# The powers of a block-diagonal inverse held as 16 columns a row, spread to 128 behind the last product

## What is computed

```python
def rwkv7_scan(r, decay, k, v, kk, a):
    def step(S, inp):
        r_t, w_t, k_t, v_t, kk_t, a_t = inp
        sa = jnp.einsum('bhij,bhj->bhi', S, -kk_t)
        S = (S * w_t[:, :, None, :]
             + sa[..., None] * (kk_t * a_t)[:, :, None, :]
             + v_t[..., None] * k_t[:, :, None, :])
        y = jnp.einsum('bhij,bhj->bhi', S, r_t)
        return S, y
```

## Time and profile before

| what | value |
|---|---|
| median of 3 runs | 1010.13 us (1010.09 to 1010.5) |
| the profiled execution | 1011.37 us, span 1009.5 us |
| TensorE matmuls | 942.1 us busy, 93% |
| TensorE weight loads | 847.1 us, 84% |
| VectorE | 574.7 us, 57% |
| ScalarE | 452.3 us, 45% |
| GpSimd | 74.9 us, 7% |
| granted TensorE clock, mean | 0.977 |
| the inverse's products | about 381 to 445 us |

### The profile page before, as it was taken

One profiled execution on the slowest core, in us unless ns is written; L12 is line 12 of the kernel. 1 busy time (PEld: TensorE's weight loads), 2 busy tenths in 40 slices (PEclk: granted clock), 3 DMA queues, 4 the chain that ended last, 5 costly groups with the idle time before them and its releaser, 6 DMA issues.

```text
span 1009.5 us, 16945 instructions
## 1 busy us (share of the span) xinstructions
PE 942.1 (93%) x7262; PEld 847.1 (84%) x7262; DVE 574.7 (57%) x706; ACT 452.3 (45%) x621; POOL 74.9 (7%) x150
## 2 busy tenths in 40 slices
PE   4999999998979998999899999997999699999995
PEld 3898889998779987887689999996985589999994
DVE  4456677556567767735475555546541865555553
ACT  5445555434356644430264444444521654435441
POOL 6000000000120012000000000000542000000000
PEclk9999999999899999989999999998999899999998
DMA  9754444556544551000155565654772156556521
GB/s 304 241 172 147 146 144 150 167 169 207 178 151 150 181 168 43 2 1 2 43 167 195 188 202 168 203 184 130 222 225 79 61 177 201 188 191 202 170 84 42
DMA packets 105642, 152.52 MB, mean 151 GB/s; under 512 B 4050, under 2 KB 82272, under 8 KB 105568
## 3 DMA queue, kind: packets, MB, share of 16 engines
q1 hardware_dynamic: 101120, 141.45, 43.2%
q0 software_dynamic: 4272, 9.85, 3.5%
q10 hardware_dynamic: 176, 0.14, 0.0%
HBM read 145.58 MB, written 1.06 MB: 145 GB/s over the span
## 4 chain that ended last, share of the span: by engine, by line
PE 85%; DVE 5%; ACT 4%; issue 3%; DMA 1%; POOL 0%; POOLq 0%; SPq 0%; ACTq 0%; DVEq 0%
PE banks L1671 23%; PE banks L1672 23%; PE banks L1673 23%; PE banks L2006 4%; PE banks L2205 3%; DVE wl L1035 2%; ACT wh L625 1%; PE banks L2094 1%; DMA raw<-in_w_in 1%; PE banks L1784 1%; DVE xl L1083 1%; PE banks L2105 1%; DMA arena<-in_l_rel_bias 1%; PE banks L1808 1%; PE banks L1759 1%
## 5 line engine op out<-in xcount | busy, mean ns | idle before, releaser
L1035 DVE TENSOR_TENSOR wl<-raw,wh 128x2048 fp32r<-128x2048 f32 x132 | 302.4, 2292 | 176.2 <-ACT wh L625 175.1
L1671 PE MATMUL banks<-xh,wh 128*128 128x256 f32 x1216 | 344.9, 284 | 2.8 <-DVE xl L1083 2.6
L1672 PE MATMUL banks<-xl,wh 128*128 128x256 f32 x1216 | 342.3, 282 | 0.0
L1673 PE MATMUL banks<-xh,wl 128*128 128x256 f32 x1216 | 342.0, 281 | 0.0
L625 ACT ACTIVATE wh<-raw 128x2048 fp32r<-128x2048 f32 x132 | 252.2, 1912 | 137.5 <-PE banks L1673 133.8
L1671 PEld LDWEIGHTS banks<-xh,wh 128*128 128x128 f32 x1216 | 230.3, 189 | 9.0 <-issue 7.8
L1672 PEld LDWEIGHTS banks<-xl,wh 128*128 128x128 f32 x1216 | 230.0, 189 | 1.4 <-issue 0.2
L1673 PEld LDWEIGHTS banks<-xh,wl 128*128 128x128 f32 x1216 | 230.4, 189 | 0.0
L1671 PE MATMUL banks<-wh,yh 128*128 128x512 f32 x288 | 114.7, 398 | 3.0 <-DVE yl L1519 3.0
L1673 PE MATMUL banks<-wh,yl 128*128 128x512 f32 x288 | 113.4, 394 | 0.0
L1672 PE MATMUL banks<-wl,yh 128*128 128x512 f32 x288 | 113.4, 394 | 0.0
(11 more groups left out here) (311 smaller groups left out, 1062.3 us busy)
## 6 DMA issues: line engine op xcount, KB each, us to landing
raw<-in_l_ffn_up SPq DMA_DIRECT2D x32, 1024.0 KB, 5.4
raw<-in_l_ffn_down SPq DMA_DIRECT2D x32, 1024.0 KB, 5.0
raw<-in_w_in SPq DMA_DIRECT2D x29, 1024.0 KB, 5.3
raw<-in_l_w_in SPq DMA_DIRECT2D x13, 1024.0 KB, 5.2
raw<-in_l_pw SPq DMA_DIRECT2D x12, 1024.0 KB, 5.5
arena<-arena POOLq DMA_DIRECT2D x64, 71.0 KB, 3.2
raw<-in_w_out SPq DMA_DIRECT2D x4, 1024.0 KB, 5.1
raw<-in_l_w_out SPq DMA_DIRECT2D x4, 1024.0 KB, 5.2
```

The costliest lines, as they stand in the source:

```text
L1035: nc.vector.tensor_tensor(wl[:, u % WBUFS, :], raw[:, u % RAWS, :], wh[:, u % WBUFS, :].bitcast(F32), ALU.subtract).then_inc(E("lo_split"), 1)
L1671: mm(out, hh, mh, start=start, stop=False)
L1672: mm(out, hh, ml, start=False, stop=False)
L1673: return mm(out, hl, mh, start=False, stop=stop)
```

## The change

The series is no longer a 128x512 tile but 128x64 in the first columns of `ts[4]`: for each head and row the 16 columns of the row's own block. Its start is a sum over the 8 blocks of `ts[0]` (all but one of them zero) into 64 columns, and an add of a 16-column identity. X2, X4 and X8 multiply the same 128x128 weights with 16 columns a head, and VectorE adds 128x64. Behind X8 the sum is spread to 128 columns a head by a multiplication with a block mask, into `ts[3]`, which held D2; Z1 and ZZ use `ts[3]`. Two constants of 24 columns together are added.

```diff
--- before.py
+++ after.py
@@ -78,6 +78,8 @@
     put("up32", same32 & (i < j))
     put("upinc32", same32 & (i <= j))
     put("eye32", (i % 32) == np.arange(32)[None, :])
+    put("eye16", (i % 16) == np.arange(16)[None, :])
+    put("block16", (i // 16) == np.arange(8)[None, :])
     keep = at
     t = np.arange(T)[None, :]
     for w in POOL_WINDOWS:
@@ -406,6 +408,13 @@
                 for places in ((slot(2), kHat, bHat), (slot(9), oslot(2), extra_t.rearrange("p i n -> p (i n)")))]
         WT = chunks(slot(2))
 
+        def series(ts):
+
+            return ts[4][:, 0:64].rearrange("p (h j) -> p h j", h=4)
+
+        def cols16(ap):
+            return ap[:, 0:64].rearrange("p (h j) -> p h j", h=4)
+
         def products(g):
 
             return slot((7, 9, 8, 12)[g])
@@ -1392,6 +1401,9 @@
                 else:
                     mark(ins)
 
+            eyes = const("eye16").rearrange("p (o j) -> p o j", o=1).broadcast_to([P, 4, 16])
+            blocks = const("block16").rearrange("p (o b i) -> p o b i", o=1, i=1).broadcast_to([P, 4, 8, 16])
+
             def heads_between(turn):
 
                 if turn in HEAD_TURNS:
@@ -1426,12 +1438,19 @@
                             masked(ts[1], use, "low16")
                         elif name == "D2":
                             nc.vector.tensor_copy(ts[3], bank(use)).then_inc(empty(use), 1)
-                        elif name in ("X2", "X4", "X8"):
+                        elif name in ("X2", "X4"):
                             if name == "X2":
                                 dve.wait_ge(E("series_begun"), g + 1)
                             else:
-                                wait_empty(dve, f"X{int(name[1]) // 2}_{g}")
-                            nc.vector.tensor_tensor(ts[4], ts[4], bank(use), ALU.add).then_inc(empty(use), 1)
+                                wait_empty(dve, f"X2_{g}")
+                            nc.vector.tensor_tensor(series(ts), series(ts), cols16(bank(use)), ALU.add).then_inc(empty(use), 1)
+                        elif name == "X8":
+                            wait_empty(dve, f"X4_{g}")
+                            mark(nc.vector.tensor_tensor(series(ts), series(ts), cols16(bank(use)), ALU.add))
+                            sync()
+                            wide = series(ts).rearrange("p h (o j) -> p h o j", o=1).broadcast_to([P, 4, 8, 16])
+                            nc.vector.tensor_tensor(ts[3].rearrange("p (h b j) -> p h b j", h=4, b=8), wide, blocks, ALU.mult)\
+                                .then_inc(empty(use), 1)
                         elif name == "ZZ":
                             tt, par = divmod(g, 2)
                             wait_empty(dve, f"Z1_{g}")
@@ -1443,8 +1462,10 @@
                         for g in (2 * pair, 2 * pair + 1):
                             ts = tset[g % 2]
                             wait_empty(dve, f"GN_{g}")
-                            idb = ident.rearrange("p (o t) -> p o t", o=1).broadcast_to([P, 4, P])
-                            nc.vector.tensor_tensor(four(ts[4]), four(ts[0]), idb, ALU.add).then_inc(E("series_begun"), 1)
+                            mark(nc.vector.tensor_reduce(series(ts), ts[0].rearrange("p (h b j) -> p h j b", h=4, b=8),
+                                                         AX_X, ALU.add))
+                            sync()
+                            nc.vector.tensor_tensor(series(ts), series(ts), eyes, ALU.add).then_inc(E("series_begun"), 1)
                         if pair == 0:
                             next_unit()
                     heads_between(len(INVERSE) * pair + i)
@@ -1998,11 +2019,14 @@
                                 ins = mm(out[:, i * HD:(i + 1) * HD], m(ts[3]), Vn[:, tt, h * HD:(h + 1) * HD],
                                          start=True, stop=True)
                             elif name == "Z1":
-                                ins = mm(o.rearrange("p (w d) -> p w d", w=2), m(ts[4]), Z[:, :, tt, h, :],
+                                ins = mm(o.rearrange("p (w d) -> p w d", w=2), m(ts[3]), Z[:, :, tt, h, :],
                                          start=True, stop=True)
+                            elif name in ("X2", "X4", "X8"):
+                                power = {"X2": 3, "X4": 1, "X8": 5}[name]
+                                ins = mm(out[:, i * 16:(i + 1) * 16], m(ts[power]), series(ts)[:, i, :], start=True, stop=True)
                             else:
-                                lhs, rhs = {"N2": (1, 0), "D2": (0, 1), "N4": (3, 5), "X2": (3, 4), "D4": (5, 3),
-                                            "X4": (1, 4), "D8": (0, 1), "X8": (5, 4), "EZ": (2, 0), "ZZ": (4, 1)}[name]
+                                lhs, rhs = {"N2": (1, 0), "D2": (0, 1), "N4": (3, 5), "D4": (5, 3),
+                                            "D8": (0, 1), "EZ": (2, 0), "ZZ": (3, 1)}[name]
                                 ins = mm(o, m(ts[lhs]), m(ts[rhs]), start=True, stop=True)
                         give(ins, f"{name}_{g}")
                     turn = len(INVERSE) * pair + at
```

## The result

The changed kernel takes 1016.39 us (median of 5 runs, 1014.76 to 1018.92) beside 1010.5 us (median of 5, 1010.09 to 1014.1) of the kernel before: the ratio is 1.0054, with a 95% interval of 1.0028 to 1.008. Two runs of the experiments fell in a slower state of the chip (1036.25 us of e11 at a clock of 0.951, 1015.67 us of e16 at 0.958) and are left out of all medians and mean clocks. The prediction had +1.4 us and 1013.8 us as its upper end.

The account below looks back on a forecast made before the run. The prediction took TensorE's issue rate, and VectorE's queue at a few places, to bound the edited stage. Products 0, series' starts +0.88 and work behind X8 +0.52 made +1.4 us on 1010.13, giving 1011.5 us, range 1009.9 to 1013.8.

Parts of the forecast that it names:

- The tiles' places: SBUF tiles behind the longer constants move by 96 bytes; no row prices this, taken as 0 us.
- The start of the series: One wide add per group becomes reduction, wait and small add on VectorE: +0.44 us a pair, +0.88 us in all.
- rival (c): At the series' start, the reduction over short runs costs double: +4.0 us, 1014.1 us; chance 0.06.
- The narrow products: X2, X4 and X8 with 16 instead of 128 columns: weight loads set the pace, so 0 us for 96 matmuls.
- AV's row: Profile row of a half-width product, 8 weight loads in 0.97 us, used to claim narrower X products gain nothing.
- rival (b): X2, X4 and X8's narrow products issue faster, at most 4.8 us off, 1006.7 us; chance 0.07.
- Behind X8: One add becomes small add, wait and spread, delaying Z1 by +0.26 us a pair, +0.52 us in all.
- The lower end of +0.2: Low end for the work behind X8, if a 16-column product's tail is shorter by 0.1 us.
- The sum of the stage: Inverse stage's terms, 0 for products, +0.88 for the series' starts, +0.52 behind X8: 1.4 us longer.
- VectorE's queue ahead of D2's copies: In pair 0, N4 waits for D2's copy behind VectorE's queue, so the 3.15 us TensorE hole becomes 3.6.
- the adds behind X2 and X4: Eight VectorE adds shrink, freeing 3.8 us that nobody waits for: 0 us on the path.
- Rival (a): TensorE's clock falls over the narrow products or longer hole: 1013.1 us with one fall, 1014.7 with two; chance 0.14.

Follow-up runs that it names:

- e11: Changed kernel with 64 unused bytes a partition behind its longer constants; 1012.5 us, median of 11 runs.
- e16: Changed kernel with 192 unused bytes behind the constants, pair 0's weight split moved behind Z1 and the series' starts behind D2's copies; 1000.7 us.
- e1_pad96: Kernel before with 96 unused bytes behind the constants, so later tiles lie where the changed kernel has them; 1014.8 us.
- e7: e2 with the reduction over 8 neighbouring elements instead of 8 lying 64 bytes apart (a different sum); 1010.4 us, one run.
- e2: Changed kernel with all tiles but vt back at the places of the kernel before, vt moved behind arena; 1015.6 us.
- e15: Changed kernel with 192 unused bytes behind the constants; 1006.6 us, median of 10 runs.
- e12: Kernel before with 32 unused bytes behind the constants; 1000.2 us, median of 4 runs.
- e3: Kernel before with VectorE's weight split of pair 0 issued two products later, behind Z1; 1006.6 us.

## Why the prediction was wrong

**The tiles' places: the step that failed.** "All tiles behind them in SBUF move by 96 bytes; no row prices this, I take 0." The measured price is +3.2 us at equal clock for e1_pad96, 3.0 by the medians, and the spacing of 120.87 instead of 119.35 ns would allow 5.5; the 1.9 us that the matmuls of 512 columns give back are part of the difference. The price is more than half of the result, and alone more than the whole forecast. Without it, the stage's +2.4 us would have made some 1012.5 us, inside the range up to 1013.8. A term that no row prices had neither bounds nor a rival, though a range was asked for. What the page could have said: 3648 matmuls read the tiles that move, so 0.1% of their pace is 0.4 us, and any effect of the places counts 3648 times.

The Trainium skill, "SBUF — State Buffer", section "SBUF: two separate sides", has it that TensorE has ports of its own and never waits on anyone. Here the two tiles that TensorE reads at once change its pace by 4.1 ns of 117, by their distance alone; the section speaks of waits on other engines, which this does not touch, and says nothing of the places of two tiles that one engine reads.

**The start of the series: right place, wrong size.** Predicted +0.44 us a pair. Measured: in pair 0, N4's start relative to N2's moved by +0.83 us (6.96 to 7.79), in pair 1 the path from the series' start to the reciprocal went from 1.20 to 2.39 us, +1.19. The mis-sized term is the reduction, 1.02 us instead of 0.65. The slope of the earlier trace rows was sound for neighbours (0.677 in e7), and what it left out is the stride. Two reductions give 2 x 0.37 = 0.74 more than the 0.44 predicted, 1.18, which is pair 1's figure. In pair 0 the split gives 0.2 back, and the first of the replaced adds had lasted 0.85 us and not 0.69. By the prediction's own sign, a reduction above 1 us, rival (c) came in, with 1.57 times 0.65 us and not the double, and for another reason: it named the short runs, and e7 shows the stride. The small add (0.22 us) and the wait in between were right.

The Trainium skill, "SBUF — State Buffer", section "Specifications (TRN2)", gives cachelines of 16 bytes and asks for two hits a line for full bandwidth. A read with 64 bytes between its elements has one hit a line, and 1.02 against 0.677 us agrees with that in sign; the page gives no price.

**The narrow products: right.** Eight loads 0.97 us, no gain from 96 matmuls of an eighth of the columns. AV's row was a good stand-in, and rival (b) is false.

**Behind X8: nearly right.** Small add 0.22 and spread 0.69 us as predicted. The delay of Z1 is +0.17 us a pair and not +0.26: from the first of X8's eight loads to VectorE's start it is 1.11 us instead of 1.19, so the narrow product's result is there 0.08 us earlier. The lower end of +0.2 had been drawn from just this.

**The sum of the stage**: predicted 1.4, by steps 0.83 + 1.19 + 2 x 0.17 = 2.36, and 2.2 by the stage's length. e2 at equal clock (+2.4) and e15 against e12 (+2.7, give or take 1.8) agree. With the stream's +3.2 that makes 5.6 us, which is the measured difference at equal clock.

**What held.** Both readings on which the mechanism rested held: VectorE's queue ahead of D2's copies is on the path (e3, e7), and nobody waits for the adds behind X2 and X4, whose 3.8 us of saved VectorE time bought nothing.

**Rival (a), the clock.** The measured kernels before and after have one mean clock, so at these distances it decides nothing. At the fast distance it costs some 3.7 us on the medians (6.4 less 2.7). Its condition, a longer half-clock stretch over the narrow products, is there in one profile, e15's; the cause stays open, as said.

## What to carry to other kernels

A change that lengthens one tile moves all that lie behind it; where a long stream reads two tiles at once, run the kernel before with an unused tile of the same length, and some other lengths, before anything is put down to the edit itself. A work step is priced from a row with the same access pattern, not only the same size, and a shorter operand gains nothing where the weight loads set the pace. Times that differ by their granted clock are put on one clock first; here 0.001 of mean clock was worth 0.72 us, nearly a third of the stage's cost.

## What was not expected of the hardware

- TensorE's pace in a stream of 128x128 weights and 256 columns depends on the distance between the tile of the weights and the tile of the moving operand, and a period of 256 bytes fits all kernels here: 116.8 to 117.7 ns at a remainder of 192, 118.7 and 118.8 at 64, 119.3 at 224, 119.4 to 119.5 at 160, 120.3 at 128, 120.9 at 0. Over 3648 matmuls the best and the worst are 15 us apart. Why was not shown; that both operands' reads meet in the same part of the memory would be a guess.
- With the tiles in the other roles (weights from xh or xl, 512 columns of wh or wl) the remainder that is worst above is the best: 228.9 to 229.2 ns at 0, against 234.9 at 160.
- A reduction on VectorE from 512 to 64 elements takes 0.677 us over neighbours and 1.02 us over elements 64 bytes apart.
- A matmul of 16 columns behind a 128x128 weight load costs what one of 128 columns does, 0.111 us.
- The same kernel runs at mean clocks from 0.973 to 0.983 (e16) on one chip, 996.5 to 1003.9 us; another, e12, at 0.981 in each of four runs.
